# Pairing the first two projection panels behind norms, and spreading the value products of an attention, in a four-layer fp32 transformer kernel

## What is computed

```
first block, layer 0:  h, hc = modulate(norm(x)), modulate(norm(ctx))
                       mixer A: 16 query heads of 64, 4 key heads, window of 128 tokens,
                       latent queries also read all 256 context keys, one sink per head;
                       context queries read context keys; y = (o * silu(g)) @ w_o
             layer 1:  mixer B: latent attention (ranks 256 and 128), keys of latents and context
                       final rmsnorm
second block, layer 0: even mixer: 8 heads of chunked attention (E) and a gated recurrence (hgrn2)
                       conv_ffn: (gelu(conv3(u)) * v) @ w_down, u, v = y @ w_up, 2816 wide
             layer 1:  odd mixer: 16 heads of chunked attention with relative bias (O), conv_ffn
rms_norm before each mixer and each ffn, and on each of their results in the second block
```

## Time and profile before

| | us |
|---|---|
| median of 3 runs | 2505.94 |
| lowest and highest run | 2505.3, 2506.0 |
| the profiled execution | 2503.26 |
| its span, first to last instruction | 2501.4 |

### The profile page before, as it was taken

The page is one execution under the profiler, slowest core; times in us unless marked ns, Lnnn a source line. Parts: engine busy times, 40 slices in busy tenths (PEclk is TensorE's granted clock), DMA queues, the critical chain, the costliest instruction groups (busy, mean ns, idle before and its releaser), DMA issues.

```text
span 2501.4 us, 30795 instructions
## 1 busy us (share of the span) xinstructions
PE 2299.5 (92%) x11952; PEld 1765.9 (71%) x11960; DVE 1034.2 (41%) x1732; ACT 873.4 (35%) x1618; POOL 688.1 (28%) x409
## 2 busy tenths in 40 slices
PE   6999888898999999897889999999997888999996
PEld 5788555587655555785677888887895566888885
DVE  2420666613165531644534524243106724425242
ACT  2322555413354431345113323233226633323231
POOL 1221000112100000440532444442443332444441
PEclk8899999997999999998888999999999989999998
DMA  6121222213100001330021333331331121333331
GB/s 245 55 63 43 85 85 77 60 43 101 42 1 1 1 24 44 90 88 17 1 59 44 100 100 92 90 100 57 93 97 31 35 60 50 94 102 91 95 95 49
DMA packets 255749, 168.70 MB, mean 67 GB/s; under 512 B 5760, under 2 KB 247143, under 8 KB 254455
## 3 DMA queue, kind: packets, MB, share of 16 engines
q1 hardware_dynamic: 251792, 157.31, 21.2%
q0 software_dynamic: 2192, 8.45, 1.1%
q10 hardware_dynamic: 1623, 0.98, 0.1%
HBM read 164.57 MB, written 2.14 MB: 67 GB/s over the span
## 4 chain that ended last, share of the span: by engine, by line
PE 78%; DVE 10%; issue 6%; ACT 3%; POOL 2%; DMA 0%; ACTq 0%; DVEq 0%; POOLq 0%
PE ps L345 18%; PE ps L347 17%; PE ps L346 17%; PE ps L427 6%; PE ps L533 4%; PE ps L372 3%; PE ps L499 3%; DVE MX L440 1%; PE ps L1236 1%; DVE SQ L1863 1%; PE ps L478 1%; POOL WL L1126 1%; PE ps L892 1%; PE ps L400 1%; PE ps L899 1%
## 5 line engine op out<-in xcount | busy, mean ns | idle before, releaser
L1126 POOL TENSOR_TENSOR WL<-raww,WH 128x1024 fp32r<-128x1024 f32 (+1 forms) x239 | 573.6, 2404 | 1062.2 <-ACT WH L300 1037.0
L345 PE MATMUL ps<-HH,WH 128*128 128x512 f32 (+1 forms) x1368 | 530.4, 388 | 34.6 <-DVE HL L1874 18.9
L346 PE MATMUL ps<-HL,WH 128*128 128x512 f32 (+1 forms) x1368 | 524.3, 383 | 0.0
L347 PE MATMUL ps<-HH,WL 128*128 128x512 f32 (+1 forms) x1368 | 523.5, 383 | 0.0
L345 PEld LDWEIGHTS ps<-HH,WH 128*128 128x128 f32 x1368 | 262.4, 192 | 102.6 <-issue 19.9
L347 PEld LDWEIGHTS ps<-HH,WL 128*128 128x128 f32 x1368 | 263.0, 192 | 49.0
L300 ACT ACTIVATE WH<-raww 128x1024 fp32r<-128x1024 f32 (+1 forms) x239 | 245.1, 1032 | 147.9 <-PE ps L347 147.8
L346 PEld LDWEIGHTS ps<-HL,WH 128*128 128x128 f32 x1368 | 263.5, 193 | 45.5
L452 ACT ACTIVATE PB<-ps,NB 128x256 f32<-128x256 f32 (+5 forms) x256 | 167.7, 655 | 112.2 <-DVE NB L441 70.4
L499 PE MATMUL ps<-ident,PB 128*128 128x128 f32 x952 | 158.6, 283 | 22.1 <-DVE PT L516 10.1
L533 PE MATMUL ps<-PT,ARENA 128*64 128x512 f32 (+3 forms) x688 | 147.4, 523 | 12.9 <-DVE PT L516 7.0
(11 more groups left out here) (254 smaller groups left out, 3403.8 us busy)
## 6 DMA issues: line engine op xcount, KB each, us to landing
raww<-in_ffn_w_up SPq DMA_DIRECT2D x88, 512.0 KB, 3.8
raww<-in_ada_w SPq DMA_DIRECT2D x32, 512.0 KB, 3.5
raww<-in_ffn_w_down SPq DMA_DIRECT2D x32, 448.0 KB, 3.7
raww<-in_odd_w_in SPq DMA_DIRECT2D x24, 512.0 KB, 3.7
raww<-in_even_w_in SPq DMA_DIRECT2D x21, 512.0 KB, 3.8
raww<-in_a_w_in SPq DMA_DIRECT2D x20, 512.0 KB, 3.8
raww<-in_ffn_w_down SPq DMA_DIRECT2D x16, 512.0 KB, 4.0
ADA<-in_ada_w SPq DMA_DIRECT2D x6, 1024.0 KB, 10.2
```

The lines of the kernel that those rows point to most:

```text
L345: nc.tensor.matmul(out, lh, rh, start=start and k == ks[0], stop=False)
L346: nc.tensor.matmul(out, lh, rl, start=False, stop=False)
L347: ins = nc.tensor.matmul(out, ll, rh, start=False, stop=stop and k == ks[-1])
L1126: nc.gpsimd.tensor_tensor(lo, raw_slot(k), hi.bitcast(F32), ALU.subtract).then_inc(*split_lo.mark(k))
```

## The change

Three parts.

*Pairs.* `lin_pair` takes the first two panels of a start together. It waits for both low parts, claims a bank for each panel and segment (four with context, two without) and then goes through the chunks: behind `h_made` k come chunk k's products of both panels and all segments. It is used at all six starts: two "ak" panels, "ckv" with "kr", "ek" with the first "eq", "u" with "v" in both feed-forwards, the first two "ok". For "ek" with "eq" the four e_q panels move ahead of e_v in the panel order, and ACT splits one more panel before the norm's first chunk.

*Attention A.* Latent heads use buffers 0 and 2, both context heads share buffer 1 (second one 256 columns further). The latent pair's value products go over four steps from z+3, those of a context pair start at its z+5 over two steps. The last pair stays as it was.

*Splits.* DVE's low parts in `pair_prep` (A and E), and the query's in O, move from i == 0 to i == 1.

```diff
         cols("e_k", we, 512, 1)
+        cols("e_q", we, 0, 4)
         for hf in range(2):
             panel(("e_v", 0, hf), we[hf * 512:(hf + 1) * 512, 640:768], 4, P)
-        cols("e_q", we, 0, 4)
...
-                if r >= 3:
-                    e.wait_ge(*pv_made[A["name"], (r - 3) | 1])
-                dst = PT[(r + 1) % 3][:, blks[0]:blks[0] + len(blks), i * P:(i + 1) * P]
+                if A["pt_free"](r) > 0:
+                    e.wait_ge(*pv_made[A["name"], A["pt_free"](r)])
+                n, q0 = A["pt"](r)
+                dst = PT[n][:, blks[0]:blks[0] + len(blks), q0 + i * P:q0 + (i + 1) * P]
...
             def dve_step_(dve, n, i):
                 m, s = step(n)
-                if m is not None and i == 0:
+                if m is not None and i == 1:
                     pair_q_low(dve, A, m, s)
...
-                over_ = jobs[r + 1]["nq"] if r + 1 < len(jobs) else 1
-                over_ = min(over_, n)
+                late, over_ = A["pv_plan"](r) if r + 1 < len(jobs) else (3, 1)
                 for g in range(over_):
-                    A["pv_at"].setdefault(z + 3 + g, []).append((r, n * g // over_, n * (g + 1) // over_))
+                    A["pv_at"].setdefault(z + late + g, []).append((r, n * g // over_, n * (g + 1) // over_))
...
+                                      "pt": lambda r: ((0, 0), (2, 0), (1, 0), (1, C))[r % 4],
+                                      "pt_free": lambda r: (r - 4) | 1,
+                                      "pv_plan": lambda r: (3, 4) if r % 4 == 1 else (5, 2),
...
+        def lin_pair(pe, two, h_, segs, ready):
+
+            outs = []
+            for stage, key, m, reader_of in two:
+                pe.wait_ge(*split_lo[key,])
+                for name, r0, nr in segs:
+                    b = lin_bank((stage, m, name))
+                    claim(pe, b, reader_of(m, name))
+                    outs.append((stage, key, m, name, r0, nr, b))
+            for k in range(8):
+                pe.wait_ge(*ready(k))
+                for stage, key, m, name, r0, nr, b in outs:
+                    wh, wl = parts_of(key)
+                    ins = split_product(ps[:, b, 0:nr], lambda k: (wh[:, k, :], wl[:, k, :]), h_(r0, nr), [k],
+                                        k == 0, k == 7)
+                    if k == 7:
+                        ins.then_inc(*grouped.mark(stage, m, name))
+            for stage, key, m, _ in two:
+                last_use(key, stage, m, segs[-1][0])
...
-            for m in range(2):
-                lin(pe, "ak", ("a_k", m), m, h_at, BOTH,
...
+            lin_pair(pe, [("ak", ("a_k", m), m,
+                           lambda m, s: (act_out, ("raw", "ak", m)) if s == "lat" else (act_out, ("akc", m)))
+                          for m in range(2)], h_at, BOTH, lambda k: h_made["n0", k])
...
-            ahead(act, ("e_k", 0), 0)
+            ahead(act, ("e_k", 0), 1)
```

More of the change, by code:

```diff
@@ L532, in att_pv @@
                     p0 = HD * (h % 2)
-                    ins = nc.tensor.matmul(ps[p0:p0 + HD, 7, a:z], v, PT[(h + 1) % 3][:, blk, a:z], start=(q == 0),
+                    at, q0_ = A["pt"](h)
+                    ins = nc.tensor.matmul(ps[p0:p0 + HD, 7, a:z], v, PT[at][:, blk, q0_ + a:q0_ + z], start=(q == 0),
                                            stop=(q == n - 1), skip_group_check=True)
@@ L657, in finish_att @@
             jobs = A["jobs"]
+            A.setdefault("pt", lambda r: ((r + 1) % 3, 0))
+            A.setdefault("pt_free", lambda r: (r - 3) | 1)
+            A.setdefault("pv_plan", lambda r: (3, 4))
             A["seq"] = [(r, i) for r, job in enumerate(jobs) for i in range(job["nq"])]
@@ L664, in finish_att @@
                 n = len(jobs[r]["pv"])
-                over_ = jobs[r + 1]["nq"] if r + 1 < len(jobs) else 1
-                over_ = min(over_, n)
+                late, over_ = A["pv_plan"](r) if r + 1 < len(jobs) else (3, 1)
                 for g in range(over_):
-                    A["pv_at"].setdefault(z + 3 + g, []).append((r, n * g // over_, n * (g + 1) // over_))
+                    A["pv_at"].setdefault(z + late + g, []).append((r, n * g // over_, n * (g + 1) // over_))
                 A["rcp_at"][z + 2] = r
                 A["spread_at"][z + 3] = r
-                A["keep_at"][z + 3 + over_] = r
+                A["keep_at"][z + late + over_] = r
             A["steps"] = max(A["keep_at"]) + 1
@@ L1005, in o_prep_dve @@
             o0 = HD - p0
-            if i == 0:
+            if i == 1:
                 dve.wait_ge(*act_out["oh", m])
@@ L1283, in mixer_b_pe @@
         def mixer_b_pe(pe):
-            lin(pe, "ckv", ("b_ckv", 0), 0, h_at, BOTH, lambda m, s: (act_out, ("ckv", s)), ready=lambda k: h_made["n1", k])
-            lin(pe, "kr", ("b_kr", 0), 0, h_at, BOTH, lambda m, s: (act_out, ("kr", s)))
+            lin_pair(pe, [("ckv", ("b_ckv", 0), 0, lambda m, s: (act_out, ("ckv", s))),
+                          ("kr", ("b_kr", 0), 0, lambda m, s: (act_out, ("kr", s)))], h_at, BOTH,
+                     lambda k: h_made["n1", k])
             for m in range(2):
@@ L1324, in even_pe @@
         def even_pe(pe):
-            lin(pe, "ek", ("e_k", 0), 0, h_at, LAT, lambda m, s: (act_out, ("raw", "ek", 0)),
-                ready=lambda k: h_made["s00", k])
+            lin_pair(pe, [("ek", ("e_k", 0), 0, lambda m, s: (act_out, ("raw", "ek", 0))),
+                          ("eq", ("e_q", 0), 0, lambda m, s: (act_out, ("raw", "eq", 0)))], h_at, LAT,
+                     lambda k: h_made["s00", k])
+            for m in range(1, 4):
+                lin(pe, "eq", ("e_q", m), m, h_at, LAT, lambda m, s: (act_out, ("raw", "eq", m)))
             lin_rows(pe, "ev", "e_v", 0, P, range(4), lambda t: (act_out, ("ev", t)))
-            for m in range(4):
-                lin(pe, "eq", ("e_q", m), m, h_at, LAT, lambda m, s: (act_out, ("raw", "eq", m)))
             for m in range(4):
@@ L1416, in ffn_pe @@
             for what, i in ffn_order():
+                if what == "up" and i == 0:
+                    lin_pair(pe, [(f"u{l}", ("up_u", l, 0), 0, lambda m, s: (act_out, ("u", l, m))),
+                                  (f"v{l}", ("up_v", l, 0), 0, lambda m, s: (dve_out, ("prod", l, m)))], h_at, LAT,
+                             lambda k: h_made[before, k])
+                    continue
                 if what == "up":
-                    lin(pe, f"u{l}", ("up_u", l, i), i, h_at, LAT, lambda m, s: (act_out, ("u", l, m)),
-                        ready=(lambda k: h_made[before, k]) if i == 0 else None)
+                    lin(pe, f"u{l}", ("up_u", l, i), i, h_at, LAT, lambda m, s: (act_out, ("u", l, m)))
                     lin(pe, f"v{l}", ("up_v", l, i), i, h_at, LAT, lambda m, s: (dve_out, ("prod", l, m)))
@@ L1440, in odd_pe @@
         def odd_pe(pe):
-            for m in range(8):
-                lin(pe, "ok", ("o_k", m), m, h_at, LAT, lambda m, s: (act_out, ("ok", m)),
-                    ready=(lambda k: h_made["s10", k]) if m == 0 else None)
+            lin_pair(pe, [("ok", ("o_k", m), m, lambda m, s: (act_out, ("ok", m))) for m in range(2)], h_at, LAT,
+                     lambda k: h_made["s10", k])
+            for m in range(2, 8):
+                lin(pe, "ok", ("o_k", m), m, h_at, LAT, lambda m, s: (act_out, ("ok", m)))
             for i in range(4):
@@ L1584, in scalar_program @@
             ahead(act, ("e_k", 0), 3)
+            for m in range(4):
+                if m:
+                    act.wait_ge(*dve_out["roped", "eq", m - 2] if m >= 2 else dve_out["roped", "ek", 0])
+                copy_out(act, raw[(m + 1) % 2], ("eq", m, "lat"), ("raw", "eq", m))
+                ahead(act, ("e_q", m), 3)
             for t in range(4):
@@ L1587, in scalar_program @@
             ahead(act, ("e_v", 0, 1), 3)
-            for m in range(4):
-                act.wait_ge(*dve_out["roped", "eq", m - 2] if m >= 2 else dve_out["roped", "ek", 0])
-                copy_out(act, raw[m % 2], ("eq", m, "lat"), ("raw", "eq", m))
-                ahead(act, ("e_q", m), 3)
             for m in range(4):
```

6 lines of the change are left out of this document (2 added, 4 removed).

## The result

| | before | after |
|---|---|---|
| median (lowest to highest) | 2505.62 (2504.99 to 2506.0) | 2460.24 (2458.62 to 2462.16) |
| profiled execution | 2503.26 | 2462.16 |
| its span | 2501.4 | 2460.3 |

The changed kernel is faster: the ratio of its time to that of the kernel before is 0.9819, 95% interval 0.9802 to 0.9836, so 1.8% less, well clear of the noise. That is 45.4 us by the medians and 41.1 by the two profiled executions, against 50.9 forecast. The runs of the kernel before are four here, one more than ahead of the prediction. The total lies well inside the range. Its parts hold up less well: two terms of attention A were wrong in opposite directions, and three waits that the sum lacks came up.

What follows compares the result with a forecast made beforehand. TensorE, busy 92% of 2501.4 us, bounds the kernel, leaving its idle time and clock to gain. 18.4 + 8.5 + 21 + 3 = 50.9 us off 2505.94 gives 2455 us, range 2442 to 2477.

Steps and rivals of the forecast that it cites:

- Large starts: First two-panel stretches behind two norms, 28.3 us each: pairing the panels gives 19.1 us, 9.2 less in each, 18.4 together.
- an earlier start moves all of it: Behind the first start PE is busy 150.87 of 150.87 us up to attention A, so the start's whole gain carries through.
- Small starts: The four other starts, one segment each: pairing gains 1.6, 1.6, 2.7 and 2.6 us, 8.5 together.
- Attention A: Moving DVE's low query part a tile later removes a stall: 19 us in six patterns, 2 in the first, 21 together.
- So I add nothing: Attention A: spreading value products puts about 1 us of PE work into small-tile steps; its cost is taken as zero.
- E, 3: Attention E: six operations cost at most 0.9 us each, half showing in PE; gain 3 us, bounds -1 and 6.
- O, 0: Attention O: the 1.80 us stall for the last low key part keeps its place; gain 0, bounds -2 and 4.
- (1): Starts: the clock does not follow, staying at 1.2 GHz as pairs change PSUM banks; 2516 us, chance 0.04.
- (2): Attention A keeps its stalls because the next release is late too; 2476 us, chance 0.12.
- (3): Large starts gain half, the clock staying low for 12 us or chunks coming slower; 2462 to 2469 us, chance 0.10.
- (4): Gain handed back at the next wait, WL or first attention operands; only A, E and a third left; 2473, chance 0.05.
- (5): Whole kernel: the change does nothing; 2506 us, chance 0.03.

Runs made afterwards that it cites:

- the starts' experiment: Changed kernel with row-projection banks claimed tile by tile and ACT's high parts of e_k and first e_q made before the norm's squares: 2450.0 us, ratio 0.9786.

## Why the prediction was right, and where it wasn't

**Large starts, 18.4 forecast.** The pair lasts 19.1 us (first product at 64.50, the last ends at 83.6) and 19.57, as worked out: 9.2 and 8.8 us less. The guess on which it stood, 5 us at 1.2 GHz, was near: in the first start the 512-column products change from every 0.43 us to every 0.23 at 69.1, 4.6 us after the first. The second stage kept it and gained 10.4; the 1.6 above 8.8 are clock behind the start. The first kept only 5.1. The step that failed is "an earlier start moves all of it" from the earlier trace rows: PE had no idle time behind the start because the banks came free one by one. The pair fills four at once. The 2.62 us of wait and the low clock behind it are what the starts' experiment got back (4.4).

**Small starts, 8.5.** Three are as worked out: 13.72 for 13.7, 13.66 for 13.6, 12.61 for 12.6. The feed-forward's fifth panel kept its 0.7 us to spare: PE waits nowhere over 0.4 us in either feed-forward up to the next norm. The bound of +3.5 each should have been 4.2 by its own terms (15.2 less 11.0); nothing hung on it. The second stage gained 2.6, the first only 0.3, since 3 us more of low clock fell into it. "ek" with "eq" took 13.21 for 12.9, but the sum priced the second WL at 0.3 beside the second chunk, and its cost lies elsewhere: `lin_pair` waits for both low parts before its first product, so the second WL of some 2.5 us (two take 5.10) stands on the path, and 2.3 of it show in the wait. I had looked at what runs beside the rounds and not at what the first one waits for.

**Attention A, 21.** Measured 21.0, but by two errors that cancel. The splits were under-sized: 27.2 in place of 21. Of the 21, 13 were to be idle time and 8 clock; measured with the splits alone were 11.8 and 15.4, because the clock then hardly falls at all (low 3.3 us in place of 36.7). The 0.30 read from the last pattern as PE's wait is the gap before its value products; the turn that waits 1.71 us in the earlier trace rows stands there at 473.00 with no wait, which carries the argument better:

```profile
473.00 0.38 PE L499 MATMUL ps<-ident,PB 128*128 128x128 f32 x2
```

I had compared with the last pattern as a floor of 27.2 us; the inner patterns with the splits alone take 26.4 (132.10 / 5). "So I add nothing" for the spreading failed: it cost about 6, of which the subtract explains 3.1 and the low clock most of the rest. I had weighed where PE's work goes, not that the kept result moves with it, two steps later, into the step of GpSimd's product. The rows for that price were in hand: the HL of 2.42 us beside WL. "No PE wait over 1 us for PT" was wrong too; there are eight, of 1.00 to 1.79 us.

**E, 3.** Idle time fell by 4.5 us, and low clock rose by 3.4, so 3.5. That the number came out is luck: the splits alone gave 8.1 here and the pairs, which change nothing here, 3.4. The mechanism is seen in the idle time alone. **O, 0.** Measured -1.4, within the bound of -2. The wait for the low key part grew to 2.45 from 1.80, as others shrank; PE's idle time in O stayed (28.5 and 28.6), so the 1.4 are clock.

**Rivals.** (1) is out: the pair changes banks every three matmuls and the clock rose all the same. By the rule of the Trainium skill that was weighed for it (TensorE: Matmul & The Clock Gate, section "A second HAM failure mode: psum-queue depth-cycling") the clock would have swung there; the trace doesn't agree, with the pace at 0.23 us from 69.1 us on. The section tells of bf16 products with short idle times of PE between groups, and the pair has none (19.57 us busy of 19.57), so its case was not met here. (2) is out: PE's idle time in A fell from 40.8 to 29.3 us, though waits for PT are left. (3) is half the truth for the first start, for another reason than the clock. (4) "handed back at the next wait" named the right kind of loss, but it was 4 us at the first start and 2.3 at "ek", not two thirds. (5) is out by the ratio.

The 9.8 us between forecast and profiled gain: first start -4.1, wait at "ek" -2.3, feed-forwards -1.3, O -1.4, A's output projection -0.9, the rest of the stage of B -1.5; second start +1.2, E +0.5.

## What to carry to other kernels

When work is bundled, read the two edges of the bundle, not its inside alone: what all of it must wait for before the first product, and what it fills at once that the next stage claims. When work is moved, list what moves with it, and put beside each of these what GpSimd or DVE, whichever is the other, does in the new step. And measure the parts alone even if the sum is right; one part of this change cost about 6 us in attention A, and one added wait took 4.4 of them away.

## What the runs showed of the hardware

A DVE operation that begins while GpSimd's is under way ended 0.54 us after GpSimd's end, in a pair where GpSimd lost nothing: 1.12 us for 0.69. A wait on GpSimd's queue that put its product behind DVE's cost nothing here: the product still lasted 0.73 us, and A fell from 220.5 to 216.1.

The granted clock is part of every stage's time and differs with the stage's own instructions unchanged. B's stage took 326.7, 325.0 or 323.8 us with 15.7, 12.1 or 6.4 us at 1.2 GHz, and E's 64.9 or 61.4 with 27.3 or 23.9. Why it fell where it did is open. A gain of 2 to 4 us in a stage is shown only where idle time or an operation's duration moved with it.
